# An expert kernel's weight loads in half slots, a split moved behind the last outputs, and output weights loaded in pieces

## The reference

```python
    return jnp.concatenate([y_a, y_b], axis=-1) @ w_out          # even mixer: (512, 1024) @ (1024, 1024)

def hierarchical_moe(x, w_rg, b_rg, w_re, b_re, w_gate, w_up, w_down):
    ...                                  # one group, then two of its 8 experts for each token
    def expert_block(args):
        xb, e = args
        hid = jax.nn.silu(xb @ w_gate[e]) * (xb @ w_up[e])      # (rows, 1024) @ (1024, 512), twice
        return hid @ w_down[e]                                  # (rows, 512) @ (512, 1024)
    ...                                  # weighted by the gates and added to x
```

## Time and profile before

| | us |
|---|---|
| median of 3 runs | 1702.59 |
| lowest and highest run | 1699.58, 1703.32 |
| the profiled execution, whole | 1702.99 |
| its span in the profile | 1700.7 |
| PE busy in the span | 1666.5 (98%) |
| PE weight loads busy | 1074.4 (63%) |
| DVE busy | 669.2 (39%) |
| ACT busy | 425.5 (25%) |
| POOL busy | 221.8 (13%) |
| moved by DMA | 460.67 MB, mean 271 GB/s |

### The profile page before, as it was taken

How to read it: one execution, slowest core, us unless ns; L and a number is a source line. 1 busy time by engine, 2 the same in 40 slices (tenths; PEclk the granted TensorE clock), 3 DMA queues, 4 the chain that set the end, 5 groups by cost and what they waited for, 6 DMA issues and landing times.

```text
span 1700.7 us, 23354 instructions
## 1 busy us (share of the span) xinstructions
PE 1666.5 (98%) x9463; PEld 1074.4 (63%) x9463; DVE 669.2 (39%) x1203; ACT 425.5 (25%) x820; POOL 221.8 (13%) x153
## 2 busy tenths in 40 slices
PE   7999999999999999998999999999999999999998
PEld 6877888754545454445888888888844454545443
DVE  3887764522423333233413223132623232423333
ACT  4566553310111001012342322323511010110110
POOL 1500001000000000001643442442100000000000
PEclk9999999999999999999999999999999999999999
DMA  9410212699999999996322122122499999999996
GB/s 203 104 50 1 52 51 100 244 425 428 427 426 428 427 427 425 429 424 263 110 98 80 70 99 100 50 99 79 179 408 426 424 425 428 427 429 429 426 429 284
DMA packets 69020, 460.67 MB, mean 271 GB/s; under 512 B 5696, under 2 KB 31520, under 8 KB 42560
## 3 DMA queue, kind: packets, MB, share of 16 engines
q1 hardware_dynamic: 68192, 457.01, 65.9%
q0 software_dynamic: 736, 2.34, 1.2%
HBM read 457.24 MB, written 2.10 MB: 270 GB/s over the span
## 4 chain that ended last, share of the span: by engine, by line
PE 92%; DMA 3%; DVE 2%; ACT 1%; POOL 1%; issue 1%; SPq 0%; DVEq 0%; ACTq 0%
PE bank L159 29%; PE bank L1817 25%; PE bank L1835 12%; PE bank L1842 7%; PE bank L1791 7%; DMA ring<-in_w_up_dram 1%; DMA ring<-in_w_in_odd_dram 1%; PE bank L2411 1%; PE bank L1826 1%; PE bank L1802 1%; PE bank L1510 1%; PE bank L947 1%; PE bank L960 1%; DMA ring<-in_w_in_even_dram 1%; POOL ring_r L2327 1%
## 5 line engine op out<-in xcount | busy, mean ns | idle before, releaser
L1817 PE MATMUL bank<-ring,SCR 128*64 128x512 f32 x2048 | 445.9, 592 | 1.4 <-issue 1.0
L159 PE MATMUL bank<-ring_r 128*128 128x512 f32 (+2 forms) x1120 | 338.1, 380 | 1.6 <-DVE ring_r L408 1.6
L1817 PEld LDWEIGHTS bank<-ring,SCR 128*64 128x64 f32 x2048 | 148.0, 137 | 291.7 <-issue 286.7
L159 PEld LDWEIGHTS bank<-ring_r 128*128 128x128 f32 x1120 | 206.2, 188 | 41.4 <-issue 2.9
L1835 PE MATMUL bank<-ring,SCR 128*64 128x512 f32 x1024 | 226.9, 595 | 0.0
L2135 DVE TENSOR_TENSOR X<-X,bank 128x512 f32<-128x512 f32 x240 | 148.3, 681 | 94.4 <-PE bank L1842 94.4
L1854 DVE SCALAR_TENSOR_TENSOR SCR<-SCR,bank 128x512 f32<-128x512 f32 x32 | 23.9, 747 | 343.6 <-PE bank L1817 343.6
L1835 PEld LDWEIGHTS bank<-ring,SCR 128*64 128x64 f32 x1024 | 70.6, 137 | 133.9 <-issue 133.9
L1842 PE MATMUL bank<-SCR_r 128*128 128x512 f32 x512 | 134.9, 406 | 6.8 <-DVE SCR_r L1851 6.8
L159 PE MATMUL bank<-ring_r,SCR_r 128*128 128x512 f32 x576 | 138.5, 395 | 0.0
L2327 POOL TENSOR_TENSOR ring_r<-ring,ring_r 128x1024 fp32r<-128x1024 f32 x48 | 117.4, 2478 | 147.8 <-ACT ring_r L2313 147.8
(11 more groups left out here) (436 smaller groups left out, 1727.2 us busy)
## 6 DMA issues: line engine op xcount, KB each, us to landing
ring<-in_w_gate_dram SPq DMA_DIRECT2D x64, 2048.0 KB, 14.2
ring<-in_w_up_dram SPq DMA_DIRECT2D x60, 2048.0 KB, 17.3
ring<-in_w_down_dram SPq DMA_DIRECT2D x60, 2048.0 KB, 14.7
ring<-in_w_in_odd_dram SPq DMA_DIRECT2D x8, 2048.0 KB, 9.6
ring<-in_w_in_even_dram SPq DMA_DIRECT2D x16, 512.0 KB, 6.6
ring<-in_w_up_dram SPq DMA_DIRECT2D x8, 1024.0 KB, 17.8
ring<-in_w_down_dram SPq DMA_DIRECT2D x8, 1024.0 KB, 15.9
ring<-in_w_in_odd_dram SPq DMA_DIRECT2D x8, 1024.0 KB, 7.8
```

Of the source, the lines that this page charges most:

```text
L159: mm = pe.matmul(out, lhs[a], rhs[b], start=(first and i == 0), stop=(last and i == 2))
L1817: mm = pe.matmul(bank[SLOTS * u:SLOTS * u + SLOTS, :], xt[:, k, SLOTS * u:SLOTS * u + SLOTS], w[u][:, k, :], start=(k == 0), stop=(k == KT ...
```

## The change

Three things are changed. Up and down weights come in half slots in all pairs of both layers, with the order and the semaphores that pair 15 had, and `up` and `down` wait for the halves in every pair; the loads of pairs 1 to 15 now all stand in the loop. ACT's first two split quarters of the odd weights stand behind both upper halves of the last pair, and DVE's first lower quarter stands behind its fourth last addition. The even output weights come as eight DMAs of 256 KB and four of 512 KB, and SP issues each piece when the one before it has landed.

```diff
--- before.py
+++ after.py
@@ -194,10 +194,10 @@
             chunks.append([(lambda s, i=i: s.rearrange("p (k s n) -> p k s n", k=KT, s=4)[:, :, i, :], src[:, :, i, :]) for i in range(4)])
         chunks += [[]] * 2
         c_oute = len(chunks)
-        chunks.append([(lambda s, g=g: s.rearrange("p (k n) -> p k n", k=4)[g * ADH:(g + 1) * ADH],
-                        w_out_even[0, g * 256:(g + 1) * 256, :].rearrange("(j d) n -> d j n", d=ADH)) for g in range(2)])
-        chunks.append([(lambda s: s.rearrange("p (k n) -> p k n", k=4),
-                        w_out_even[0, 512:1024, :].rearrange("(p k) n -> p k n", p=P))])
+        chunks.append([(lambda s, g=g, j=j: s.rearrange("p (k n) -> p k n", k=4)[g * ADH:(g + 1) * ADH, j, :],
+                        w_out_even[0, g * 256 + j * ADH:g * 256 + (j + 1) * ADH, :]) for j in range(4) for g in range(2)])
+        chunks.append([(lambda s, k=k: s.rearrange("p (k n) -> p k n", k=4)[:, k, :],
+                        w_out_even[0, 512:1024, :].rearrange("(p k) n -> p k n", p=P)[:, k, :]) for k in range(4)])
         c_moe = [len(chunks)]
         for i in range(NE // 2):
             chunks += [[None]] * 6
@@ -1867,8 +1867,8 @@
         def first_half(q):
             return sg(("up_half", "down_half")[q // 2 - 1])
 
-        def w_half(l, q, a):
-            return w_need(l, q, PAIRS - 1) if a else (first_half(q), 32 * (l + 1))
+        def w_half(l, q, i, a):
+            return w_need(l, q, i) if a else (first_half(q), 32 * PAIRS * l + 32 + 32 * i)
 
         def w_two(l, q, k):
             return [slot_of(c_moe[l] + q + u).rearrange("p (k n) -> p k n", k=k) for u in range(2)]
@@ -1905,10 +1905,7 @@
                 hidden_mm(pe, BG, range(2), w_two(l, 0, KT), x_of(n), ready).then_inc(ms("gate"), 1)
 
             def up(i, n):
-                if is_at(i, last):
-                    ready = [(a * KT // 2, w_half(l, 2 + u, a)) for a in range(2) for u in range(2)]
-                else:
-                    ready = [(0, w_need(l, 2 + u, i)) for u in range(2)]
+                ready = [(a * KT // 2, w_half(l, 2 + u, i, a)) for a in range(2) for u in range(2)]
                 hidden_mm(pe, BU, range(2), w_two(l, 2, KT), x_of(n), ready).then_inc(ms("up"), 1)
 
             def hidden_t(i):
@@ -1918,10 +1915,7 @@
                 ht_mm(pe).then_inc(ms("ht"), 1)
 
             def down(i):
-                if is_at(i, last):
-                    ready = [(a * 2, w_half(l, 4 + u, a)) for a in range(2) for u in range(2)]
-                else:
-                    ready = [(0, w_need(l, 4 + u, i)) for u in range(2)]
+                ready = [(a * 2, w_half(l, 4 + u, i, a)) for a in range(2) for u in range(2)]
                 if not is_at(i, 0):
                     pe.wait_ge(*mw("y_lower", 2 * i))
                 pe.wait_ge(*mw("ht_out", i + 1))
@@ -2047,8 +2041,8 @@
                     if not is_at(i, 0):
                         act.wait_ge(*mw("comb", 8 * i))
                     y_upper(act, half).then_inc(ms("y_upper"), 1)
-                    if l == 0 and is_at(i, last) and upto > 2 and half == 0:
-                        split_act(act, 0, (0, 1))
+                if l == 0 and is_at(i, last) and upto > 2:
+                    split_act(act, 0, (0, 1))
 
             for q in range(4):
                 act.wait_ge(*mw("gat", q + 1))
@@ -2125,8 +2119,6 @@
                         add_last(0, LAST_ORDER[0])
                     dve.wait_ge(*mw("y_upper", 2 * i + half + 1))
                     y_lower(dve, half).then_inc(ms("y_lower"), 1)
-                    if l == 0 and is_at(i, last) and upto > 2 and half == 0:
-                        split_lower(dve, 0, (0,))
 
             def add(i, m):
                 dve.wait_ge(*mw("comb", 8 * i + m + 1))
@@ -2173,6 +2165,8 @@
             pairs_loop(dve, pair)
             for n in range(1, 8):
                 add_last(n, LAST_ORDER[n])
+                if l == 0 and n == 3 and upto > 2:
+                    split_lower(dve, 0, (0,))
             with dve.If(most[0] > SLOTS):
                 dve.wait_ge(*mw("added", 8 * PAIRS))
                 with dve.Fori(1, SEQ // SLOTS) as b:
@@ -2217,21 +2211,21 @@
                 c = c_moe[l] + q
                 half = slice(a * SLOT // 2, (a + 1) * SLOT // 2)
                 if a == 0:
-                    sp.wait_ge(*freed(l, q, i))
-                src = mats[q // 2].rearrange("e (p k) n -> p e (k n)", p=P)[:, 2 * i + q % 2, half]
-                sp.dma_start(slot_of(c)[:, half], src).then_inc(w_landed[c % RING] if a else first_half(q), 16)
-
-            for q in range(6):
-                load(0, q)
-            with sp.Fori(1, PAIRS - 1) as i:
-                for q in range(6):
+                    sp.wait_ge(*(released[c - RING] if is_at(i, 0) else freed(l, q, i)))
+                src = mats[q // 2].rearrange("e (p k) n -> p e (k n)", p=P)[:, one(2 * i + q % 2), half]
+                sp.dma_start(slot_of(c)[:, half], src.rearrange("p e n -> p (e n)")).then_inc(w_landed[c % RING] if a else first_half(q), 16)
+
+            def loads(i):
+                for q in range(2):
                     load(i, q)
-            for q in range(2):
-                load(PAIRS - 1, q)
-            for m in (2, 4):
-                for a in range(2):
-                    for u in range(2):
-                        load_half(PAIRS - 1, m + u, a)
+                for m in (2, 4):
+                    for a in range(2):
+                        for u in range(2):
+                            load_half(i, m + u, a)
+
+            loads(0)
+            with sp.Fori(1, PAIRS) as i:
+                loads(i)
 
         def overflow_sp(sp, l, usual=None, behind=None):
             ms = lambda n: moe_sem(l, n)
@@ -2654,7 +2648,9 @@
                     sp.wait_ge(sg("a_proj"), 8)
                 elif c >= RING:
                     sp.wait_ge(*released[c - RING])
-                for dst, src in chunks[c]:
+                for i, (dst, src) in enumerate(chunks[c]):
+                    if i and c in (c_oute, c_oute + 1):
+                        sp.wait_ge(w_landed[c % RING], landed(c) - 16 * (len(chunks[c]) - i))
                     sp.dma_start(dst(slot_of(c)), src).then_inc(w_landed[c % RING], 16)
 
             for c in range(c_moe[0]):
```

## The result

The changed kernel takes 1708.55 us (median of 6 runs, 1706.34 to 1709.65), the kernel before in the same comparison 1702.74 us. The ratio is 1.0033 with a 95% interval of 1.0021 to 1.0045: 5.8 us slower. The forecast was 1706.3 us, in a range of 1697.5 to 1713. The profiled executions tell the same: a span of 1706.7 us where the earlier trace rows have 1700.7, so 6.0 us more.

The account below looks back on a forecast made before the run. Expert stages were taken to end with a continuous DMA stream, PE needing nearly the same time. Terms -3.6 - 1.1 + 8.4 = +3.7 us gave 1706.3 us against a median of 1702.59; range 1697.5 to 1713.

Parts of the forecast that it names:

- part 1, stream: Expert stages: 8 KB packets lengthen the continuous stream by 0.15 us per two halved slots, +4.2 us a layer, 8.4 both.
- clock behind the last gate waits: Last pair's gate product, both layers: the prediction had no term for PE's clock falling there.
- part 2: End of layer 0: the 5.89 us stall goes, POOL's quarters come next, the clock falls behind them; -1.1 us.
- part 3: Even mixer: PE's 1.78 us stop and its half clock go, the eighth piece's lateness cuts the gain to -3.6 us.
- What bounds the kernel: Expert stages: a continuous stream of bytes at about 427 GB/s, not PE, sets each stage's end, one for one.
- waits at gate in the later pairs: Expert stages: a sign that the forecast is right, with both stages 4 us longer and the up wait gone.
- Rival (b): Layer boundary: the clock holds, 2.8 us less, 1703.5 us in all, no change that can be told; chance 0.22.
- the forecast's fear: Layer boundary: after three idle pieces PE runs at 1.2 GHz behind POOL's last quarter, giving 2.8 us back.
- the 3.35 us of the clock: Even mixer: without the stop the clock should not fall, 3.35 us more beside the stop's 1.8, 5.1 before the cut.

Follow-up runs that it names:

- E5: Changed kernel, loads still in halves, but up and down wait for all four halves except in the last pair: 1705.80 us, ratio 1.0012 to the kernel before.
- E1: Kernel before with only the half slots and their waits in every pair: 1711.87 us, ratio 1.0052.
- E2: Kernel before with only the odd-weight splits moved behind the last outputs: 1699.93 us, ratio 0.9984.
- E3: Kernel before with only the even output weights in pieces, each issued behind the last one's landing: 1700.89 us, ratio 0.9989.
- E6: Changed kernel with the down weights of pairs 0 to 14 whole again, half as many halved loads: 1702.81 us, ratio 0.9998 to the kernel before.
- E7: Changed kernel with both experts' halves in one 2 MB DMA where slots are neighbours, packets still 8 KB: 1708.41 us, ratio 1.0028 to the kernel before.
- E4: Kernel before with the moved odd splits and the even pieces, without half slots: 1698.09 us, ratio 0.9976.
- E8: Kernel before with moved odd splits and even pieces, the pieces issued two at a time: 1695.50 us, ratio 0.9958.
- E9: E8 with one quarter of the first odd weights' lower bits moved from POOL to DVE: 1694.01 us, ratio 0.9945 to the kernel before.
- E10: Kernel before, with only the second 1 MB load of the first even output chunk held until the first lands: 1698.62 us, ratio 0.9970.

## Why the prediction was right, by its steps

The forecast held in sign, range and size, 2.2 us short. By its terms:

| us | forecast | in the profiles | by the runs |
|---|---|---|---|
| part 1, stream | +8.4 | +7.5 | |
| clock behind the last gate waits | 0 | +3.2 | +3.6 (E5) |
| part 1 in all | +8.4 | | +8.9 (E1) |
| part 2 | -1.1 | -4.3 | -2.7 (E2) |
| part 3 | -3.6 | -2.6 | -1.9 (E3) |
| odd mixer | 0 | +1.6 | |
| the end | 0 | +0.6 | |
| sum | +3.7 | +6.0 | +5.8 |

**What bounds the kernel** was right for the stage's end. Pair periods, the rate and the last gate wait all moved as a continuous stream says. The "waits at gate in the later pairs" came too, but small: PE has some 4 us of margin that the stream uses up first, the periods are 29.45 to 29.68 us from the tenth or eleventh pair on, where PE alone needs 29.39, and only the last stop is long.

**Part 1's stream term** was right in mechanism and near in size. Over 14 pairs 3.68 and 3.83 us are 0.13 us for two halved slots, where I took 0.15 (bounds 0.11 and 0.3). E6 shows the dose, E7 that it is the packet. The rate over the long stretches fell by 0.7 and 0.9%, and the stage up to gate 15 grew by 0.85 and 0.88%. That the price came so near is in part luck. Windows of 7 us over whole slots in the kernel before read anything from 419 to 433 GB/s (500 to 507 us, 540 to 547 us), so the 424, 424 and 419 of the earlier trace rows do not tell half slots from whole ones; only the landings, 0.3 us good to 0.15, were evidence. The Trainium skill, "DMA: Bandwidth & Descriptors", section "Why small descriptors are slow", would have had 1.7 us a layer (my estimate from it in the prediction); the trace has 3.7 to 3.8, so here the measurement decides, and its rule stands in direction only.

**The term that was missing** is what the late gate does to the clock. I had written that the clock fell behind stops of 5.89 and 1.78 us, used that at the boundary, and did not ask it of the stop that my own part 1 was making: a stream 4.2 us longer meets a PE that is not slower, so the last gate must wait about 4 us more. It did (3.85 and 3.88 us), the clock went to 1.2 GHz for 3.4 us, and gate 15 took 1.70 and 1.52 us longer. E5 takes away the single stop and keeps the stream, and the 3 us go; E6 shortens the stop, and they go too. This is the step of the prediction that failed: a cost put at nothing without a reason, of 3.2 to 3.6 us.

**Part 2**: the chain was right step by step (0.92 us wait, POOL's three quarters next, two waits of PE for them), and the size was wrong. The clock held through the three idle pieces, so the gain is not 1.1 us. It was to be 3.9 us in that case (805.58 to 801.8 is 3.8); the boundary shortened by 2.5 us in E2, 3.2 in E4 and 4.3 in the changed kernel. Most of it is the clock and not the idle time: the twelve products alone take 5.49 us before and 3.00 in E4, while PE has new waits for POOL in place of the 5.89 us. The split is tied to the landing of the odd weights, and where the last down product stands against the landing differs: from its start to ACT's split are 10.6 us before, 11.7 in E2 and 8.4 in the changed kernel, where PE itself is late. Part of the 4.3 us is thus part 1's loss given back: E1 has 1.6 us of it with the splits where they were. Rival (b), the clock holds at the boundary, was the true one for this step in the changed kernel, E2, E4, E8 and E9. In the profile of E5 the clock does fall behind the same two waits for POOL, and the boundary takes 47.39 us, so the forecast's fear was not empty.

**Part 3**: the stop was a fetch and went, and ACT waited for the eighth piece: both as written. A piece took 3.5 us on average, not 3.3. What was too large is the 3.35 us of the clock in the gain. It stood on one window of one execution; E1 and E2 have the same stop with the clock at full, and the mean clocks of the timed runs put it at 1.7 to 2.3 us (E3, E4). The sum by these numbers, 1.8 us of stop and about 2 of clock less 1.9 for the eighth piece (E3), is near 2 us; the runs show 1.9 us with an interval of 0.2 to 3.6. The -2.6 us in the profiles is not this part's alone. By the place where PE's timelines drift apart, the old stop and its half clock cost 5.0 us before and the eighth piece 1.9 us after, so part 3 brought 3.1 us there; another 1.2 us are an earlier start, and a half clock at 170 us, 20 us before the changed loads are issued, takes 1.7 us back. How much such things move a profile is shown by E8 and E9: they have the same code up to the first gate product and start it at 322.32 and 320.18 us, 1.5 of these 2.1 us behind a half clock at 311 us in E8. The Trainium skill's formula in "DMA: Bandwidth & Descriptors", section "Anatomy of one DMA", is given there for transfers that GpSimd issues, while SP issues these. The trace of the changed kernel bears out that a piece is mostly fixed time, but not the 2.6 us estimated from the formula: a piece into 64 partitions takes 3.3 to 3.8 us.

**The rest**: in the changed kernel the clock fell once more, at 828.7 us in the odd mixer, 1.6 us. The last section comes back to that. The 0.6 us at the end I cannot place.

So the forecast came out close partly because errors of both signs met: 3.2 us of clock missing and 1.6 us by chance on one side, some 3 us too little gain at the boundary on the other, of which at least 1 us is part 1's loss given back.

## What to carry to other kernels

Where transfers run without a pause and PE keeps up with them only just, the size of a packet is a price on the whole stage: halving 16 KB packets to 8 KB on two thirds of the bytes took 0.9% of it, and an earlier start of the products bought nothing. When a longer stream and an unchanged engine meet, work out where the engine's waiting will collect, and whether its clock survives a stop of that length; the same loss in small waits was 3 us cheaper. Take a term for the clock from more than one profile, or from the mean clock of many runs: one window of one execution was 1 to 1.7 us off here. And a rate read over a few microseconds scatters by more than the effect looked for. A stop of PE with no releaser, while large loads are queued, is a reason to look at the instruction queue: holding back one load cured it.

## What the runs showed of the hardware

- At the last gate product the clock held at full behind stops of 2.34 and 2.59 us (E6), and fell at those of 3.79 to 3.89 us, in both layers (after, E1, E7), between 0.4 us before their end and 1.1 us behind it. Each of these falls lasted 3.4 us and cost 1.5 to 1.7 us. It fell for 6.8 us at the stops of 4.51 to 6.42 us in the boundary (before, E1, E3, E10).
- Behind stops of 1.3 to 2.2 us in the even mixer it held six times: old stop, 1.50 and 1.36 us (E1, E2); eighth piece, 1.78, 1.91, 1.33 and 2.17 us (after, E3, E4, E7). It fell once, for 6.8 us behind 1.78 us (before). It also fell behind 3.49 us there (E5).
- The clock also falls without such a stop. Ahead of the first gate product seven of the twelve profiles have a fall of 3.4 us at places of their own: at 15.5 us (E3), 16 (E7), 170 (after), 241 (E2), and 311 to 313 (E1, E6, E8), the last with no stop of PE over 0.3 us in the 4 us ahead. E4, E9 and E10 have none. In the odd mixer the clock falls for 3.4 us in some executions and not in others, near 824 to 832 us, near 1214 to 1224 us, or at both. Ahead of the first place PE has three stops of 0.34 to 0.52 us, ahead of the second none over 0.3 us. The mixer takes 400.2 us with none (before, E3, E4, E8, E9), 401.7 to 401.8 with one (after, E1, E2), 403.1 to 403.3 with two (E5, E6, E7, E10). Each number agrees with its count of falls, and the cause is open: all kernels with halves have them, but so do E2 and E10 without.
- A packet of 16 KB takes 0.614 us and one of 8 KB 0.313 us when all 16 engines are full (after), and with the packets of two thirds of the bytes halved the stage is 0.9% longer.
- A fetch of instructions waits behind queued weights: its packet comes at 202.6 us in the kernel before, with 2 MB queued, and at 197.4 in E10, where the same products run 1.3 us earlier; some 4 us.
